# The down weights of an expert as one unit, and the memory's value weights by rows

## What is computed

```python
# 32 experts, D = 1024, D_EXPERT = 512, two experts per token; row_tok, row_w, blk_exp: the tokens sorted by expert
def expert_block(args):
    toks, wb, e = args
    xb = hf[toks]
    hid = jax.nn.silu(jnp.matmul(xb, w_g[e])) * jnp.matmul(xb, w_u[e])
    return jnp.matmul(hid, w_d[e]) * wb[:, None]
...
y = jnp.zeros_like(hf).at[row_tok].add(yb.reshape(n_rows, D))
...
# second block, memory of 256 rows
k, v = jnp.split(memn @ w_kv, 2, axis=-1)      # w_kv is 1024 x 2048; v is memn @ w_kv[:, 1024:]
```

## Time and profile before

| | us |
|---|---|
| median of 3 runs | 1024.79 |
| lowest and highest run | 1023.57, 1024.86 |
| the profiled execution | 1024.2 |
| its span, first to last instruction | 1022.4 |
| PE busy | 898.9 (88%) |
| DVE busy | 459.0 (45%) |
| ACT busy | 367.9 (36%) |
| read from memory | 298.84 MB, 293 GB/s over the span |

### The profile page before, as it was taken

The page is one execution under the profiler, slowest core; times in us unless marked ns, Lnnn a source line. Parts: engine busy times, 40 slices in busy tenths (PEclk is TensorE's granted clock), DMA queues, the critical chain, the costliest instruction groups (busy, mean ns, idle before and its releaser), DMA issues.

```text
span 1022.4 us, 14477 instructions
## 1 busy us (share of the span) xinstructions
PE 898.9 (88%) x6088; PEld 660.7 (65%) x6088; DVE 459.0 (45%) x818; ACT 367.9 (36%) x586; POOL 8.0 (1%) x14
## 2 busy tenths in 40 slices
PE   7999999999888867658676766899999999999997
PEld 7989989864246321313222231388999999999886
DVE  6899867501010010100101010189666579888842
ACT  5565585310010000101000010248655666557632
POOL 1000000000000000000000000000100000000000
PEclk9999999999899977979777797999999999999999
DMA  9856436999999999999999999982534256654541
GB/s 329 283 211 231 141 124 254 410 406 429 417 409 427 408 431 422 424 426 426 429 420 431 421 429 423 404 299 84 168 104 162 84 167 192 205 179 165 188 183 41
DMA packets 78493, 301.27 MB, mean 295 GB/s; under 512 B 4195, under 2 KB 30948, under 8 KB 62818
## 3 DMA queue, kind: packets, MB, share of 16 engines
q1 hardware_dynamic: 76640, 298.82, 74.3%
q10 hardware_dynamic: 1458, 1.07, 0.4%
q0 software_dynamic: 336, 0.53, 0.3%
HBM read 298.84 MB, written 1.05 MB: 293 GB/s over the span
## 4 chain that ended last, share of the span: by engine, by line
PE 63%; DMA 28%; DVE 4%; ACT 2%; SPq 1%; issue 1%; DVEq 0%; PEldq 0%; ACTq 0%
PE bank L1447 11%; DMA ring<-in_w_gate_e_dram 9%; DMA ring<-in_w_down_e_dram 9%; DMA ring<-in_w_up_e_dram 8%; PE bank L1103 7%; PE bank L1465 6%; PE bank L697 3%; PE bank L1327 3%; PE bank L1342 3%; PE bank L820 3%; PE bank L790 3%; PE bank L724 3%; PE bank L1161 3%; DMA qvpr<-in_w_down_e_dram 2%; PE bank L1133 2%; PE bank L979 2%
## 5 line engine op out<-in xcount | busy, mean ns | idle before, releaser
L1103 PE MATMUL bank<-ring,big 128*32 128x512 f32 x768 | 164.0, 717 | 77.4 <-DMA ring<-in_w_up_e_dram 40.2
L1103 PEld LDWEIGHTS bank<-ring,big 128*32 128x32 f32 x768 | 38.9, 127 | 194.8 <-issue 91.0
L354 DVE TENSOR_TENSOR ring_parts<-ring,ring_parts 128x2048 fp32r<-128x2048 f32 (+1 forms) x54 | 118.9, 2247 | 30.0 <-ACT ring_parts L346 29.7
L346 ACT ACTIVATE ring_parts<-ring 128x2048 fp32r<-128x2048 f32 (+1 forms) x53 | 96.7, 1874 | 46.5 <-DMA ring<-in_w_down_dram 22.4
L2372 DVE TENSOR_TENSOR xT<-bank,xT 128x512 f32<-128x512 f32 x32 | 22.1, 691 | 136.7 <-PE bank L1147 136.7
L1447 PE MATMUL bank<-mrg_parts,ring_parts 128*128 128x256 f32 x640 | 82.3, 281 | 0.0
L1447 PEld LDWEIGHTS bank<-mrg_parts,ring_parts 128*128 128x128 f32 x640 | 78.5, 189 | 0.0
L2329 DVE TENSOR_TENSOR big<-big,const 128x128 f32<-128x128 f32 x14 | 3.5, 288 | 153.7 <-PE bank L1090 153.7
L1103 PE MATMUL bank<-hs,big 128*32 128x512 f32 x128 | 67.9, 683 | 0.0
L1133 PE MATMUL bank<-ring,big 128*32 128x512 f32 x336 | 47.8, 699 | 17.4 <-DMA ring<-in_w_down_e_dram 14.6
L1103 PE MATMUL bank<-qvpr,big 128*32 128x512 f32 x112 | 60.9, 696 | 0.0
(11 more groups left out here) (458 smaller groups left out, 1641.9 us busy)
## 6 DMA issues: line engine op xcount, KB each, us to landing
ring<-in_w_up_e_dram SPq DMA_DIRECT2D x24, 2048.0 KB, 28.8
ring<-in_w_gate_e_dram SPq DMA_DIRECT2D x24, 2048.0 KB, 22.1
ring<-in_w_down_e_dram SPq DMA_DIRECT2D x17, 2048.0 KB, 21.1
ring<-in_w_in_dram SPq DMA_DIRECT2D x12, 2048.0 KB, 14.5
ring<-in_w_up_dram SPq DMA_DIRECT2D x22, 1024.0 KB, 6.6
ring<-in_w_down_e_dram SPq DMA_DIRECT2D x12, 1024.0 KB, 19.7
ring<-in_w_down_dram SPq DMA_DIRECT2D x5, 2048.0 KB, 8.0
ring<-in_w_out_dram SPq DMA_DIRECT2D x4, 2048.0 KB, 9.2
```

Of the source, the lines that this page charges most:

```text
L346: signal(act.activation(pairs[stage][u % 3][0][:, part], raws[stage][u % 3][:, part], ACT.Copy), stage + "_hi")
L354: signal(eng.tensor_tensor(lo[:, part], raws[stage][u % 3][:, part], hi[:, part].bitcast(F32), ALU.subtract), name)
L1103: mm = pe.matmul(bank[part][CAP * j:CAP * j + CAP, :], xeT[:, c, CAP * j:CAP * j + CAP], w[j][c], start=(c == 0), stop=(c == DC - 1))
```

## The change

A down unit becomes one expert's whole down matrix: partition p holds four consecutive rows, one run of 16 KB, in all steps but the last, which keeps the old units (`by_pairs`, `w_d2`). PE waits for all four down units and then does the 64 instructions in one block; each slot is given free by its expert's last matmul. Since the row order of `hidT` follows, the transposes read every fourth word of `hid` instead of every second. The halved load of the last down unit remains in the last step alone. SP's loop runs over turns 1 and 2 and further ones; the last turn is written out behind it, with the wait for `rounds`, the register load and the branch ahead of it.

The value weights are cut by rows instead of columns: unit i is rows of four of the eight chunks, all 1024 columns, in runs of 4 KB. After step 0 PE sums chunks 0 to 3 into four banks, and ACT copies the four banks to `mrg`; after step 1 it sums chunks 4 to 7, and DVE adds the four banks to `mrg`.

The core of the diff:

```diff
-            w_d = A["w_down_e"][0].rearrange("(q r j) (u p c) n -> q u r p j (c n)", r=2, j=2, c=2, p=P)
+            w_d = A["w_down_e"][0].rearrange("(q j) (p c) n -> q j p (c n)", j=QUAD, c=4)
+            w_d2 = A["w_down_e"][0].rearrange("(q r j) (u p c) n -> q u r p j (c n)", r=2, j=2, c=2, p=P)
+            def load_expert(q, s, u, by_pairs=False):
+                if not by_pairs or u < 8:
+                    sp.dma_start(expert_slots[s][:, :], (w_g, w_u, w_d)[u // 4][q, u % 4].rearrange("q p n -> p (q n)")
+                                 ).then_inc(landed[s], 16)
+                    return
...
-            def value_weights(i, ks):
-                return w_xkv[:, ks, 1024 + 512 * i:1536 + 512 * i]
+            def value_weights(ks):
+                return w_xkv[:, ks, 1024:2048]
...
-            def two_steps(q, m):
+            def two_steps(q, m, last=False):
...
-                        load_expert(bass.ds(q * 2 + step, 1), s, u, (step, u) == (1, 11))
+                        which = slice(q * 2 + step, q * 2 + step + 1) if last else bass.ds(q * 2 + step, 1)
+                        load_expert(which, s, u, last and step == 1)
...
-            with sp.Fori(1, PAIRS) as m:
+            with sp.Fori(1, PAIRS - 1) as m:
                 two_steps(m, m)
             sp.wait_ge(S["rounds"], 1)
             last_turn = sp.value_load(count_i[0:1, 0:1], min_val=PAIRS - 1, max_val=PAIRS * ROUNDS - 1)
             with sp.If(last_turn > PAIRS - 1):
-                with sp.Fori(PAIRS, last_turn + 1) as m:
+                with sp.Fori(PAIRS - 1, last_turn) as m:
                     two_steps(m % PAIRS, m)
...
+            two_steps(PAIRS - 1, last_turn, last=True)
...
-                    mm = pe.transpose(bank[7][:, P * k:P * k + P], hid[:, 256 * (k // 2) + k % 2:][:, 0:255:2], ident)
+                    rows = hid[:, 256 * (k // 2) + k % 2:][:, 0:255:2] if last else hid[:, k:][:, 0:509:4]
+                    mm = pe.transpose(bank[7][:, P * k:P * k + P], rows, ident)
...
-                for u in range(0 if last else 2):
-                    pair = [unit(8 + 2 * u + r) for r in range(2)]
-                    w = [slot[:, :].rearrange("p (j c n) -> p j c n", j=2, c=2) for slot, _ in pair]
-                    for c in range(2):
+                else:
+                    slots = [unit(8 + j) for j in range(QUAD)]
+                    for c in range(4):
                         for half in range(2):
-                            for j in range(QUAD):
-                                mm = pe.matmul(bank[2 + half][CAP * j:CAP * j + CAP, :],
-                                               hidT[:, 2 * u + c, CAP * j:CAP * j + CAP],
-                                               w[j // 2][:, j % 2, c, 512 * half:512 * half + 512],
-                                               start=(u == 0 and c == 0), stop=(u == 1 and c == 1))
-                                if c == 1 and half == 1 and j % 2:
-                                    mm.then_inc(pair[j // 2][1], 1)
+                            for j, (slot, free) in enumerate(slots):
+                                mm = pe.matmul(bank[2 + half][CAP * j:CAP * j + CAP, :], hidT[:, c, CAP * j:CAP * j + CAP],
+                                               slot[:, D * c + 512 * half:D * c + 512 * half + 512], start=(c == 0), stop=(c == 3))
+                                if (c, half) == (3, 1):
+                                    mm.then_inc(free, 1)
...
                 for t in range(TT):
-                    for k in range(8):
-                        mm = pe.matmul(bank[t][:, :], qko[:, k * T + P * t:k * T + P * t + P], w[:, k], start=(k == 0), stop=(k == 7))
-                    mm.then_inc(S["vx_full"], 1)
+                    for half in range(2):
+                        for k in range(4):
+                            mm = pe.matmul(bank[2 * t + half][:, :], qko[:, (4 * u + k) * T + P * t:][:, 0:P],
+                                           w[:, k, 512 * half:512 * half + 512], start=(k == 0), stop=(k == 3))
+                        mm.then_inc(S["vx_full"], 1)
...
+            for i in range(4):
+                dve.wait_ge(S["vx_full"], 4 + i + 1)
+                dve.wait_ge(S["vx_out"], 4)
+                v = mrg[:, 512 * i:512 * i + 512]
+                dve.tensor_tensor(v, bank[i][:, :], v, ALU.add).then_inc(S["vx_out"], 1)
```

More of the change, by code:

```diff
@@ L540, in _ @@
             w_u = A["w_up_e"][0].rearrange("(q j) (p c) n -> q j p (c n)", j=QUAD, c=8)
-            w_d = A["w_down_e"][0].rearrange("(q r j) (u p c) n -> q u r p j (c n)", r=2, j=2, c=2, p=P)
[L543 to L546, removed]
+            w_d = A["w_down_e"][0].rearrange("(q j) (p c) n -> q j p (c n)", j=QUAD, c=4)
[5 more added lines that the diff above has]
+                    return
+                to = expert_slots[s][:, :].rearrange("p (j c n) -> p j c n", j=2, c=2)
+                of = w_d2[q, u % 4 // 2, u % 2].rearrange("q p j n -> p (q j) n")
+                if u == 11:
                     for c in range(2):
                         sp.dma_start(to[:, :, c], of[:, :, D * c:D * c + D]).then_inc((S["down_half"], landed[s])[c], 16)
-                elif u < 8:
-                    sp.dma_start(expert_slots[s][:, :], (w_g, w_u)[u // 4][q, u % 4].rearrange("q p n -> p (q n)")
-                                 ).then_inc(landed[s], 16)
-                else:
-                    sp.dma_start(expert_slots[s][:, :].rearrange("p (j n) -> p j n", j=2),
-                                 w_d[q, u % 4 // 2, u % 2].rearrange("q p j n -> p (q j) n")).then_inc(landed[s], 16)
-            def value_weights(i, ks):
-                return w_xkv[:, ks, 1024 + 512 * i:1536 + 512 * i]
+                else:
+                    sp.dma_start(expert_slots[s][:, :].rearrange("p (j n) -> p j n", j=2), of).then_inc(landed[s], 16)
+            def value_weights(ks):
+                return w_xkv[:, ks, 1024:2048]
             def load_unit(step, u):
@@ L561, in load_unit @@
                 sp.wait_ge(used[s], turn + 1)
-                load_expert(slice(step, step + 1), s, u, (step, u) == (1, 11))
+                load_expert(slice(step, step + 1), s, u)
             def load_spare(i):
@@ L579, in first_turn @@
                     sp.wait_ge(S["half_used"], i + 1)
-                    w = w_d[0, (i + 1) // 2, (i + 1) % 2]
-                    sp.dma_start(expert_slots[i][:, 0:2048], w[:, 0]).then_inc(S["down_early"], 16)
+                    sp.dma_start(expert_slots[i][:, 0:2048], w_d[0, i + 1][:, 0:2048]).then_inc(S["down_early"], 16)
                 sp.wait_ge(S["keys_read"], 1)
@@ L584, in first_turn @@
                 sp.wait_ge(S["half_used"], 4)
-                sp.dma_start(expert_slots[3][:, 0:2048].rearrange("p (k n) -> p k n", k=4),
-                             value_weights(0, slice(0, 4))).then_inc(S["value_early"], 16)
+                sp.dma_start(expert_slots[3][:, 0:2048].rearrange("p (k n) -> p k n", k=2),
+                             value_weights(slice(0, 2))).then_inc(S["value_early"], 16)
                 for u in range(9, 12):
@@ L590, in first_turn @@
                     sp.wait_ge(used[s], turn + 1)
-                    w = w_d[0, (u - 8) // 2, (u - 8) % 2]
-                    sp.dma_start(expert_slots[s][:, 2048:], w[:, 1]).then_inc(landed[s], 16)
+                    sp.dma_start(expert_slots[s][:, 2048:], w_d[0, u - 8][:, 2048:4096]).then_inc(landed[s], 16)
                 for step in range(2):
@@ L598, in first_turn @@
                     sp.wait_ge(used[s], turn + 1)
-                    half = 1 - step
+                    ks = (slice(2, 4), slice(4, 8))[step]
                     assert step or s == 3
-                    sp.dma_start(expert_slots[s][:, 2048 * half:].rearrange("p (k n) -> p k n", k=8 - 4 * half),
-                                 value_weights(step, slice(4 * half, 8))).then_inc(landed[s], 16)
+                    sp.dma_start(expert_slots[s][:, (2048, 0)[step]:].rearrange("p (k n) -> p k n", k=ks.stop - ks.start),
+                                 value_weights(ks)).then_inc(landed[s], 16)
                 s, turn = KEY_UNIT
@@ L1072, in unit @@
                         pe.wait_ge(S["down_early"], 48)
-                    if (step, u) == (1, 11) and half != 1:
-                        pe.wait_ge(S["down_half"], m * 16 + 16)
+                    if half == 0:
+                        pe.wait_ge(S["down_half"], 16)
                     if half != 0:
@@ L1389, in _ @@
             small_attention("x", 0, 16, (0, 1))
-            pe.wait_ge(S["vx_out"], 4)
+            pe.wait_ge(S["vx_out"], 8)
             for h in range(2):
@@ L1724, in _ @@
                 expert_step(0, half_turn, True)
-                for t in range(TT):
-                    act.wait_ge(S["vx_full"], 2 * half_turn + t + 1)
-                    act.activation(mrg[:, t * 1024 + half_turn * 512:t * 1024 + half_turn * 512 + 512], bank[t][:, :],
```

(6 more changed lines are left out.)

6 lines of the change are left out of this document (3 added, 3 removed).

## The result

| | before | after |
|---|---|---|
| median of 20 runs each, us | 1025.77 | 1027.24 |
| lowest and highest run | 1023.57, 1028.16 | 1024.56, 1028.8 |
| ratio, 95% interval | | 1.0017, 1.001 to 1.0024 |
| the profiled execution, its span | 1024.2, 1022.4 | 1028.8, 1027.0 |

The change costs 1.5 us by the medians and 1.7 us by the ratio (1.0 to 2.5), where +3.0 had been forecast. The forecast took 0.2%, 2 us, as the least that the measurement tells from no change, and gave "slower" 0.71 and "same" 0.21. The measured 0.17% is clear of zero, but lies on the side of "same". Two runs beside the experiments, 1190.44 us with the block twice in the later steps and 1713.53 us of the kernel before, were in a slow state and are in no median or ratio of this text.

The account below looks back on a forecast made before the run. Transfers bound the expert loop, with PE level and slightly later at step 2's start. +5.5 (downs) +0.1 (adds) -2.2 (16 KB runs) -0.4 (gate) = +3.0 us on 1024.2, plus 0.6 to the median: 1027.8, range 1024.4 to 1030.3.

Parts of the forecast that it names:

- What bounds the kernel: Expert loop: transfers alone decide, except at step 2's start, where PE and transfers are level, PE slightly later.
- The block in step 1: Step 1's downs: 64 matmuls behind the last landing take 9.7 us, so PE leaves 5.5 us later (bounds 2.9 to 6.0).
- the adds: Values of step 1: adds on DVE replace copies on ACT, 0.1 us more behind the last bank.
- The 0.5 us by which the last down unit was to land earlier: Step 1: 16 KB runs let the last down unit land 0.56 us earlier, taken as 0.5.
- The 16 KB runs: Downs of steps 2 to 6: longer runs save 2.2 us of transfer time in full.
- The values and the transposes: Earlier value landings gain nothing; transposes at a step of four words cost nothing, at most 0.6 us in step 0.
- The gate of step 2: Gate matmuls of step 2: a clock fall may not recur, gain up to 1.7, loss up to 1.3, taken as -0.4 us.
- The cover of the later steps: Steps after step 1: the added wait costs nothing, since queued gate units cover it with 9 us left.
- What arrives at the end: Whatever PE loses between 289 and 336 us, ahead of step 2's down issue, arrives at the kernel's end.
- the "-2.7" of the forecast's rival: Rival: PE's extra wait decides nothing and only the transfers' gain is left, -2.7 us, 1022.1; chance 0.07.
- The +0.6 from the profiled execution to the median: Base of the forecast: the median of the runs, 1024.79, lies 0.6 us above the profiled execution, 1024.2.

Follow-up runs that it names:

- block twice in the later steps: The changed kernel with the block of 64 down matmuls done twice in steps 2 to 6; 1030.74 us, ratio to before 1.0056.
- the first experiment: The changed kernel with step 1 alone put back to down units in 8 KB runs, taken in two pairs; 1022.24 us, ratio to before 0.9983.
- values alone: The kernel before with the value weights by rows and nothing else; 1025.21 us, ratio to before 1.0004.
- The fillers: The changed kernel with seven or six unread matmuls in PE's wait for step 1's downs; 1026.35 us (ratio to before 1.0013) and 1025.28 us (1.0006).
- block in step 1 alone: The kernel before with step 1's four down units in 16 KB runs, taken together in one block; 1028.49 us, ratio to before 1.0040.
- six fillers: The changed kernel with six unread matmuls, three behind the second and three behind the third down landing of step 1; 1025.28 us, ratio to before 1.0006.
- after's second: The changed kernel once more, no edit, on another chip, with a second trace; 1026.52 us, ratio to before 1.0014.
- the block done twice: The changed kernel with its block of 64 matmuls repeated, in two kernels: in step 1, 1035.12 us (ratio to before 1.0104); in steps 2 to 6, 1030.74 (1.0056).
- before's second trace: The kernel before once more, no edit, on another chip; 1024.86 us, ratio to the other runs of before 0.9998.

## Why the forecast came out as it did

The sign and the place of the loss held, and the size was twice what was measured. The step that failed is that PE's whole loss ahead of s2 arrives at the end of the kernel. Step by step:

**What bounds the kernel: right, with one qualification.** PE and the transfers are level at s2, as rows 4 and 5 said. That PE is the later one was read from a profiled execution whose gate lost its clock. With pairs and a kept clock it is the earlier one: then no dip is seen at all (334 to 338 us of the first experiment, s1 to s2 in 70.86 us). So part of what PE loses there is first used up as slack.

**The block in step 1: right up to s2.** Forecast ahead of s2 were +5.5 for the downs, +0.1 for the adds and -0.4 for the gate, +5.2 in all. The three traces of the form of before (before twice, values alone) need 72.8 us from s1 to s2 in the mean, the two of after 77.8: +5.0. The block took 9.73 and 8.48 us (10.04 in the block alone), 9.7 was the forecast, at a clock part of the time at 1.2 GHz. The fillers show that this clock, and nothing else, stands between 7.1 and 9.7 us. The sum fits better than its terms. The 0.5 us by which the last down unit was to land earlier doesn't show: from s1 to that landing it is 25.3 us in the mean both in the three traces of before's form and in the seven with the block. Each of those three traces also has one fallen clock of its own ahead of s2 (the gate twice, the second pair once). And the idle time was 5.8 to 6.7 us in the five traces with the block and no fillers, not 5.2: the forecast counted it from the start of the first pair and left out the 0.70 us that PE had waited before that. The kernel before:

```profile
283.35 3.64 PE L1133 MATMUL bank<-ring,big 128*32 128x512 f32 x32 [0.70 <-ACT big L1713]
```

**The 16 KB runs: right.** Forecast -2.2; block in step 1 alone against after, behind s2: 319.79 against 317.80, -2.0. By the ratios the runs bring 1.7 us with pairs in step 1 and 2.4 to 2.7 with the block. A pair of steps takes 117.9 and 117.45, forecast 117.4.

**The values and the transposes: right, nothing.** Values alone 1.0004 (0.9992 to 1.0016), and the add on DVE is 0.70 us as reckoned. The transposes take 285 ns at a step of four words, 283 at two. The Trainium skill's rule that "each access that crosses to a new line pays a penalty" (SBUF — State Buffer, the note on SBUF cachelines) isn't borne out here: with every fp32 word in a 16-byte line of its own, the same instruction took 2 ns more. The measurement decides. The next sentence of that note names 4 fp32 as how far one can stride for free; if a step of four words is meant, this run agrees with it, and the forecast read only the first half.

**The gate of step 2: a coin, not a gain.** It took 8.8 to 8.9 us in 5 of the 12 traces (before, values alone, six fillers, block twice later, after's second) and about 7.2 in the others, and kernels of both forms are in both groups. The expected -0.4 can't be ascribed to the change.

**The cover of the later steps: right in effect, wrong in size.** After loses nothing there, but 4 to 6 us were left instead of 9. The forecast counted the queue's work up to the last landing; the next loads have to be issued some 5 us before it, by the estimate from the block done twice.

**What arrives at the end: the term that was mis-sized.** The forecast let the block's loss at s2 arrive in full: "Whatever PE loses between 289 and 336 us arrives at the end of the kernel", +5.2 us. Up to s2 it was +5.0, but at the end the runs show less. By the ratios the block costs 4.1 us with 8 KB runs (block in step 1 alone against before) and 3.1 to 3.5 with 16 KB runs (after against step 1 in pairs). The table says where the rest goes: behind s2 the kernels with pairs take longer than those with the block, 321.0 us in the mean against 319.79 with 8 KB runs and 319.3 against 317.8 with 16 KB runs, 1.2 and 1.5 us. With 16 KB runs this is the qualification above: where s2 comes before the transfers run out, their rest is counted behind it, and PE's first loss only uses it up. With 8 KB runs all three traces have a dip, and the same reading is argued, not shown. Beyond that the loss arrives in full, as the block done twice shows. The landings agree: around s2 the transfers fall behind a spacing of 4.89 us per unit by 1.0, 1.9 and 2.8 us in the three traces of before's form, and by 5.9 to 6.4 in three with the block (alone, and after twice), some 4 us more. Since 5.2 still lies inside the interval of the first comparison (2.9 to 5.3), the size of the part that is lost is known to about 1 us only.

The sum was made against one execution, and its agreement with that one is luck: from s1 to the loop's end before took 72.46 + 320.05 = 392.5 us, after 395.3 and 395.9, so +2.8 and +3.3 for the +3.0. The other two traces of before's form need 394.2 and 394.8 there, and the mean of the three is 393.8: against it after loses 1.8 us, near what the medians say (1.5). Partly these traces have larger gaps, as in the second trace of before, where a unit lands 6.77 us behind the one before it, at 345 us, although its issue at 336.16 was earlier than that of rows 4. Why the transfers stall longer in some executions than in others stays open: SP's issue times don't explain it.

The time itself, 1027.8 for 1027.24, came near by two errors that cancel: the change was taken 1.5 us too high, and the base, 1024.79 from three runs, was 1.0 us below the 1025.77 of the twenty. The +0.6 from the profiled execution to the median was fair: 1024.2 lies 1.6 us below that median and 0.4 to 0.8 below the other three medians of before.

**The cheaper kernel.** The first experiment takes what was right and leaves what was wrong: 16 KB runs everywhere but in step 1, where PE's order keeps 32 of the 64 instructions ahead of the last landing. Its 1022.24 us is 1.7 us under before (0.7 to 2.8) and 3.1 to 3.5 under after by the ratios. This is the "-2.7" of the forecast's rival in kind, reached by avoiding the wait instead of hiding it.

## What to carry to other kernels

A coarser wait costs the engine the work that used to run under the last transfers, and again what PE's clock loses in the idle time it opens. At the end of the kernel this arrives less the time by which the transfers were the later ones there. It is free only where the slots that it holds are wanted later than its end, and that cover has to be reckoned to the moment at which the queue thins, not to the last landing. Where two resources are level, mend the transfers and leave the order alone at that one place: the same change was a loss with the block there and a gain without. And a sum of a few us that is made against one profiled execution needs to know where that execution lies among its runs, and which of two level resources is the later one in the others.

## What was not expected of the hardware

- The length of the idle time alone doesn't settle whether the clock falls. Behind 2.74 us without work the second pair of step 1 took 5.40 us in before's second trace; behind 2.04 us in the first and 1.56 in the first experiment it took 3.64 to 3.70. The gate of step 2 follows 1.95 us of idle time in both the earlier trace rows and after's trace, and took 8.88 us in one and 7.17 in the other.
- A queue thins before its last landing: 153 GB/s from 622 to 625 us where the last unit of 2 MB landed at 625.8, although new loads had been issued at 623.32. Behind an issue into an empty queue after's stretch from 343 to 345 still shows 123 GB/s, with the issue at 343.26.
